# First units behind each norm read the unscaled stream; the norm's factor is applied to their sums

## What is computed

```python
def rmsnorm(x, w):
    y = x * rsqrt(mean(x * x, axis=-1) + EPS)
    return y * w

# A: linear attention with decays
q, fz, i, gate = split(rmsnorm(x, a_norm_w) @ a_w_in);  x = x + (o * silu(gate)) @ a_w_out
# F: keys and values from one norm weight, queries and gates from another
k, v, fz = split(rmsnorm(x, kv_norm_w) @ kv_w);  k = head_rmsnorm(k, k_norm_w)
F = cumsum(log_sigmoid(fz + f_bias))
q, gate = split(rmsnorm(x, b_norm_w) @ b_w_in);  q = head_rmsnorm(q, b_q_norm_w)
x = x + (attention(q, k, v, F) * silu(gate)) @ b_w_out
# C: recurrent unit and attention on 64 selected keys through a latent of 512
xr, q, ckv, qi, ki, wi, gr, ga = split(rmsnorm(x, norm_mix_g) @ w_in)
ckv = rmsnorm(ckv, kv_norm_g);  ki = layernorm(ki)
x = x + mixed @ w_o
# Q: product-key experts: 16 of 16384 experts for each of 8 heads
q = rmsnorm(x, norm_ffn_g) @ peer_wq;  s1, s2 = q1 @ keys1, q2 @ keys2;  top 16, gates
x = x + sum(gate * gelu(h @ u) * v);  out = rmsnorm(x)
```

## Time and profile before

| | |
|---|---|
| median of three timed executions | 3247.22 us |
| the profiled execution | 3245.94 us, its span 3244.2 us |
| PE, PEld | busy 3208.8 and 3052.5 us |
| DVE, ACT, POOL | busy 2346.5, 1671.6 and 7.7 us |
| DMA | 570 MB, 176 GB/s, 49.8% of 16 engines |
| stages (PE, us from the span's start) | start to 23.65; A to 459; OA to 551.17; F to 975; OF to 1067.84; X to 1153; C to 1590; OC to 1684.36; Q to 1787; experts to the end |

### The profile page before, as it was taken

The page is one execution under the profiler, slowest core; times in us unless marked ns, Lnnn a source line. Parts: engine busy times, 40 slices in busy tenths (PEclk is TensorE's granted clock), DMA queues, the critical chain, the costliest instruction groups (busy, mean ns, idle before and its releaser), DMA issues.

```text
span 3244.2 us, 63012 instructions
## 1 busy us (share of the span) xinstructions
PE 3208.8 (99%) x25320; PEld 3052.5 (94%) x25320; DVE 2346.5 (72%) x3759; ACT 1671.6 (52%) x2240; POOL 7.7 (0%) x27
## 2 busy tenths in 40 slices
PE   8999999999999999999999999999999999999998
PEld 7999999999999999999999999998899889987887
DVE  7777667655565675666668998975699558999865
ACT  5454544767684555556544444444444444444444
POOL 0000000000000000000000000000000000000000
PEclk9999999999999999999999999999999999999999
DMA  4444434444444454555445555555555555555554
GB/s 179 148 168 144 166 139 173 171 166 167 156 168 176 165 187 172 177 176 180 163 165 194 176 188 182 182 187 193 192 182 182 195 195 182 182 182 182 183 206 156
DMA packets 99096, 569.96 MB, mean 176 GB/s; under 512 B 9456, under 2 KB 30320, under 8 KB 31600
## 3 DMA queue, kind: packets, MB, share of 16 engines
q1 hardware_dynamic: 98928, 567.58, 49.8%
HBM read 565.45 MB, written 2.10 MB: 175 GB/s over the span
## 4 chain that ended last, share of the span: by engine, by line
PE 90%; DVE 6%; DVEq 1%; DMA 1%; ACT 1%; issue 1%; SPq 0%; ACTq 0%
PE bank L530 20%; PE bank L532 20%; PE bank L531 20%; PE bank L1039 7%; PE bank L1040 7%; PE bank L1041 7%; DVE wl L1542 2%; PE bank L965 1%; PE bank L693 1%; PE bank L879 0%; ACT wh L1070 0%; PE bank L764 0%; PE bank L765 0%; PE bank L640 0%; DMA raw<-w_out_b 0%
## 5 line engine op out<-in xcount | busy, mean ns | idle before, releaser
L530 PE MATMUL bank<-hh,wh 128*128 128x256 f32 x5680 | 1597.8, 281 | 10.9 <-DVE hl L1575 9.1
L531 PE MATMUL bank<-hl,wh 128*128 128x256 f32 x5680 | 1577.3, 278 | 0.0
L532 PE MATMUL bank<-hh,wl 128*128 128x256 f32 x5680 | 1577.3, 278 | 0.0
L1542 DVE TENSOR_TENSOR wl<-raw,wh 128x1024 fp32r<-128x1024 f32 x1052 | 1252.8, 1220 | 357.6 <-ACT wh L1070 349.4
L1070 ACT ACTIVATE wh<-raw 128x1024 fp32r<-128x1024 f32 x1052 | 1052.0, 1050 | 310.7 <-DMA raw<-w_in_a 130.8
L530 PEld LDWEIGHTS bank<-hh,wh 128*128 128x128 f32 x5680 | 1070.6, 188 | 18.5 <-issue 6.8
L531 PEld LDWEIGHTS bank<-hl,wh 128*128 128x128 f32 x5680 | 1071.8, 189 | 3.0 <-issue 1.7
L532 PEld LDWEIGHTS bank<-hh,wl 128*128 128x128 f32 x5680 | 1069.3, 188 | 0.0
L1039 PE MATMUL bank<-wh,ah 128*128 128x512 f32 x1024 | 402.0, 393 | 0.0
L1041 PE MATMUL bank<-wl,ah 128*128 128x512 f32 x1024 | 398.9, 390 | 0.0
L1040 PE MATMUL bank<-wh,al 128*128 128x512 f32 x1024 | 398.5, 389 | 0.0
(11 more groups left out here) (376 smaller groups left out, 2883.7 us busy)
## 6 DMA issues: line engine op xcount, KB each, us to landing
raw<-peer_u SPq DMA_DIRECT2D x128, 1024.0 KB, 4.9
raw<-peer_v SPq DMA_DIRECT2D x128, 1024.0 KB, 4.9
raw<-w_in_c SPq DMA_DIRECT2D x64, 1024.0 KB, 4.9
raw<-w_in_a SPq DMA_DIRECT2D x63, 1024.0 KB, 4.9
raw<-w_kv SPq DMA_DIRECT2D x32, 1024.0 KB, 4.8
raw<-w_in_b SPq DMA_DIRECT2D x32, 1024.0 KB, 4.9
raw<-w_out_a SPq DMA_DIRECT2D x16, 1024.0 KB, 4.9
raw<-w_out_b SPq DMA_DIRECT2D x16, 1024.0 KB, 4.9
```

Of the source, the lines that this page charges most:

```text
L530: eng.matmul(out, h_[:, k, :], high[:, k, :], start=(k == 0), stop=False)
L531: eng.matmul(out, h_[:, k, :], low[:, k, :], start=False, stop=False)
L532: last = eng.matmul(out, low_rows(c, k), high[:, k, :], start=False, stop=(k == KC - 1))
L1542: eng.tensor_tensor(low_half_out(c, half), raw_half(c, half), high_half(c, half).bitcast(F32), ALU.subtract).then_inc(lo_ready, 1)
```

## The change

For each norm there are now two more tiles, `unscaled[name]` (in F `kh` and `kl`): high and low parts of stream times norm weight, without the norm's factor. ACT (`unscaled_high`) and DVE (`unscaled_low`) make them pair by pair during the out-projection, at the start behind the weighing. PE takes them for the first units: four in A, in F the gates' unit and all units of keys and values of all pairs, four in X, four in Q. `norm_sum` comes between the halves of the first unit (`first_unscaled`); `two_products` is gone, and the keep-clock matmuls but for 6 at the start. The factor is applied where the sums are read: a multiplication on DVE of the two banks of A and of the queries of Q, for the gates' unit another; the values of F get it per token as `scale` of ACT's copy, from two transposes of `rstd`; keys and latent are normed anyway, so only their epsilon is divided by the squared factor: `eps_times` makes EPS/rstd^2 from the sum of squares, and DVE adds it to the sum ahead of the root, in F in each pair. In `stream_norm` the scaled parts for the later units follow, with the weights of units 3 and 4 in rounds 2 and 5. In A's first pair the low part of unit 5 stands ahead of `key_decays`, those of 6 and 7 ahead of the two parts of `query_decays`. The small chain for `lb` and `rg_c` moves from behind the first norm to the start. In C's first pair the low parts of `uk` and `uv` are made behind `xc`; in OF `f_norm` moves from chunk 0 to chunk 4 of the second unit; the first load of `uk` and `uv` waits for unit X+4.

```diff
-SPLIT_AT = {"A": 0, "F": 8, "C": 24, "Q": 32}
+SPLIT_AT = {"A": 0, "F": 8, "C": 16, "Q": 24}
...
                 eng.matmul(B[4][:, 0:T], ones[:, :], sq[:, 0, 0:T], start=True, stop=False)
-                keep_clock(3)
                 eng.wait_ge(sq_ready, 8 * NORM_AT[name] + 8)
                 eng.matmul(B[4][:, 0:T], ones[:, :], sq[:, 1, T:2 * T], start=False, stop=True).then_inc(ss_done, 1)
-                keep_clock(15)
+            def first_unscaled(name, c, out):
+                if NORM_AT[name] > 0:
+                    eng.wait_ge(x_next_to_last, NORM_AT[name])
+                product(0, c, out, *unscaled[name], (ul_ready, 8 * NORM_AT[name]), lambda: norm_sum(name))
...
-            for g in range(KC // 2):
+            for g in range(KC // 2 - 2):
                 first_norm_sum(g)
-            keep_clock(14)
+            keep_clock(6)
...
-            two_products(BASE["FG"], [B[5][:, 0:T], B[0][:, 0:T]], kh, kl, SPLIT_AT["F"])
+            first_unscaled("F", BASE["FG"], B[5][:, 0:T])
...
+                if first:
+                    for t in range(NT):
+                        last = eng.transpose(B[7][:, t * P:(t + 1) * P], rstd[:, t * P:(t + 1) * P], ident[:, :])
+                    last.then_inc(s["rtok_done"], 1)
...
-            out_projection("OF", "F", "C", 3, {(0, 6): (f_values,), (1, 0): (f_norm,)})
+            out_projection("OF", "F", "C", 3, {(0, 6): (f_values,), (1, 4): (f_norm,)})
...
-            two_products(u, [latent_bank(0), latent_bank(1)], hh, hl, SPLIT_AT["C"])
-            for c in range(2, RC):
-                product(0, u + c, latent_bank(c), hh, hl)
-            product(0, u + RC, B[2][:, 0:T], hh, hl)
+            first_unscaled("C", u, latent_bank(0))
+            for c in range(1, RC):
+                product(0, u + c, latent_bank(c), uh_c, ul_c)
+            product(0, u + RC, B[2][:, 0:T], hh, hl, (hl_ready, SPLIT_AT["C"]))
...
+            def unscaled_high(name, g):
+                eng.wait_ge(weighed, 8 * NORM_AT[name] + g + 1)
+                eng.activation(chunk(unscaled[name][0], 2 * g, 2), chunk(oT, 2 * g, 2), ACT.Copy).then_inc(uh_ready, 1)
...
+                high_part(0, NORM_UNIT[name] + 2)
+                for g in range(KC // 2):
+                    eng.wait_ge(hf_ready, SPLIT_AT[name] + g + 1)
+                    eng.activation(chunk(hh, 2 * g, 2), chunk(oT, 2 * g, 2), ACT.Copy).then_inc(hh_ready, 1)
+                    if g == 0:
+                        high_part(0, NORM_UNIT[name] + 3)
+                    if g == 3:
+                        high_part(0, NORM_UNIT[name] + 4)
...
-                rsqrt(krs[:, :], B[4][:, :], 1.0 / P).then_inc(s["krs_ready"], 1)
+                eng.wait_ge(s["kvar_ready"], i + 1)
+                rsqrt(krs[:, :], krs[:, :], 1.0 / P, None).then_inc(s["krs_ready"], 1)
...
+            def eps_times(out, n):
+                eng.tensor_scalar(out[:, :], B[4][:, 0:T], n * EPS / D, n * EPS * EPS, ALU.mult, ALU.add)
...
+                eng.wait_ge(s["kss_done"], i + 1)
+                eng.tensor_tensor(krs[:, :].rearrange("p (j t) -> p j t", j=2), B[4][:, :].rearrange("p (j t) -> p j t", j=2),
+                                  epsv_f[:, :].unsqueeze(1).broadcast_to([P, 2, T]), ALU.add).then_inc(s["kvar_ready"], 1)
...
             def a_body(i, first):
...
+                if first:
+                    key_decays(i)
+                    low_part(i, 6)
                 query_decays(i, 0, 3)
-                low_part(i, 6)
+                low_part(i, 7 if first else 6)
```

More of the change, by code:

```diff
@@ L947, in _ @@
                 outs = [query_bank(g, j)[:, j * T:(j + 1) * T] for j in range(2)]
[L948 to L952 removed]
+                for j in range(2):
+                    c = BASE["Q"] + 2 * g + j
+                    if g == 0 and j == 0:
+                        first_unscaled("Q", c, outs[j])
+                    elif g < 2:
+                        product(0, c, outs[j], uh_q, ul_q)
+                    else:
+                        product(0, c, outs[j], hh, hl, (hl_ready, SPLIT_AT["Q"]) if g == 2 and j == 0 else None)
                 if g >= 1:
@@ L1186, in a_body @@
                     eng.activation(osq_a[:, :], B[4][:, :], ACT.Square).then_inc(s["osq_ready"], 1)
-                high_part(i, 5)
-                eng.wait_ge(mm_done, after("A", i, 3))
-                if past_zero(i):
+                if not first:
+                    high_part(i, 5)
+                    eng.wait_ge(mm_done, after("A", i, 3))
                     eng.wait_ge(s["lv_done"], i)
-                eng.activation(q_a[:, :], B[1][:, :], ACT.Copy).then_inc(s["qz_ready"], 1)
+                    eng.activation(q_a[:, :], B[1][:, :], ACT.Copy).then_inc(s["qz_ready"], 1)
                 high_part(i, 6)
@@ L1310, in f_body @@
                 copy_probs(s, i, probT_f)
-                keep_values_tok(s, i, v_f)
+                if past_zero(i):
+                    eng.wait_ge(s["o_done"], i)
+                eng.wait_ge(s["vt_done"], i + 1)
+                for t in range(NT):
+                    last = eng.activation(v_f[:, t, :], B[2][:, t * G:(t + 1) * G], ACT.Copy, scale=rtok[:, t:t + 1])
+                last.then_inc(s["v_ready"], 1)
                 high_part(i, u + 10)
@@ L1573, in low @@
[L1573 to L1595 removed]
+                if name == "F":
+                    eps_times(epsv_f, P)
@@ new lines, in stream_norm @@
+                if name == "C":
+                    eps_times(epsv_c, KV_RANK)
+                low_part(0, NORM_UNIT[name] + 2)
+                eng.drain()
+                for g in range(KC // 2 + 1):
+                    if g < KC // 2:
+                        if weight is None:
+                            last = eng.tensor_tensor(oT[:, 2 * g:2 * g + 2, :], oT[:, 2 * g:2 * g + 2, :],
+                                                     rstd[:, :].unsqueeze(1).broadcast_to([P, 2, T]), ALU.mult)
+                        else:
+                            for c in (2 * g, 2 * g + 1):
+                                last = eng.scalar_tensor_tensor(out=oT[:, c, :], in0=xT[:, c, :], scalar=col(weight, c),
+                                                                in1=rstd[:, :], op0=ALU.mult, op1=ALU.mult)
+                        last.then_inc(hf_ready, 1)
+                    if g >= 1:
+                        eng.wait_ge(hh_ready, SPLIT_AT[name] + g)
+                        eng.tensor_tensor(chunk(hl, 2 * g - 2, 2), chunk(oT, 2 * g - 2, 2), chunk(hh, 2 * g - 2, 2).bitcast(F32),
+                                          ALU.subtract).then_inc(hl_ready, 1)
+                    if g == 2:
+                        low_part(0, NORM_UNIT[name] + 3)
+                    if g == 5:
+                        low_part(0, NORM_UNIT[name] + 4)
+                    if between is not None:
+                        between(g)
@@ L1722, in query_decays @@
                 if first == 0:
+                    if isinstance(i, int) and i == 0:
+                        eng.wait_ge(mm_done, 2 * (BASE["A"] + 4))
+                        eng.tensor_tensor(q_a[:, :].rearrange("p (j t) -> p j t", j=2), B[1][:, :].rearrange("p (j t) -> p j t", j=2),
+                                          rstd[:, :].unsqueeze(1).broadcast_to([P, 2, T]), ALU.mult).then_inc(s["qz_ready"], 1)
+                        eng.drain()
                     eng.wait_ge(s["qz_ready"], i + 1)
@@ L1976, in c_tail, with latent_lows @@
                 eng.tensor_tensor(chunk(oT, i * 2, 2), on_c[:, :], mixr[:, :], ALU.add).then_inc(mixed, 1)
+            def latent_lows(i):
+                for n, (low, full, high) in enumerate(((uk_l, uk, uk_h), (uv_l, uv, uv_h))):
+                    eng.wait_ge(s["kvw_high"], 2 * i + (n + 1))
+                    eng.tensor_tensor(low[:, :, :, :], full[:, :, :, :], high[:, :, :, :].bitcast(F32),
+                                      ALU.subtract).then_inc(s["kvw_low"], 1)
             def c_body(i, first, final=False):
@@ L1982, in c_body @@
                 low_part(i, u + 3)
-                for n, (low, full, high) in enumerate(((uk_l, uk, uk_h), (uv_l, uv, uv_h))):
-                    eng.wait_ge(s["kvw_high"], 2 * i + (n + 1))
-                    eng.tensor_tensor(low[:, :, :, :], full[:, :, :, :], high[:, :, :, :].bitcast(F32),
-                                      ALU.subtract).then_inc(s["kvw_low"], 1)
+                if not first:
+                    latent_lows(i)
                 eng.wait_ge(mm_done, unit(i, BASE["C"] + 1, 2, 2))
```

295 lines of the change are left out of this document (149 added, 146 removed).

## The result

The changed kernel takes 3228.32 us (median of four, 3226.40 to 3230.59) beside 3247.28 for the kernel before: a ratio of 0.9942, 95% interval 0.9929 to 0.9954. A second set of five gave 3227.43 and 0.9944 (0.9931 to 0.9958). The forecast was 3233.6. The profiled execution took 3230.59 us, its span 3228.9.

The account below looks back on a forecast made before the run. TensorE, 99% busy, was taken as the bound, with late DVE or ACT steps deciding its waits at norms. Gains of 16.1 us less 2.5 for the clock gave 13.6, hence 3233.6 us from a profiled 3245.94, range 3225 to 3242.

Parts of the forecast that it names:

- Start: A's first pair: PE's first product at about 21.5, pair ending at 72.0 against 77.49, a gain of 5.5 us.
- F: Norm of F: F+2 waits about 3 us and ends at t+27.8 instead of t+31.5, a gain of 3.65 us.
- The cover of 0.4: F's first pair: query low part ready at t+39.8, wanted by PE at t+40.2, so no loss.
- The added step in the seven later pairs: F's later pairs: the new add of 0.7 us falls in DVE's idle time and costs nothing; uncovered, 4.9 us.
- OF: Out-projection after F: moving `f_norm` 12 matmuls down fills its wait of 1.46 us, a gain of 1.4 us.
- X and Q: Norms of X and Q: PE goes on at t+32.5 and starts key_scores(0) at t+25.2, gains of 2.75 and 2.8 us.
- The waits that were named as signs: PE waits of 2 to 3 us, in X for `csq` and in Q for `keysT`, expected if the forecast was right.
- C: C's first pair: the wait of 0.97 us for `xc` goes, but that for `prob_c` grows by as much; gain 0.
- The sign named: C's first pair: PE waits 1.5 us or more for `prob_c` at L640, expected if the forecast was right.
- The clock: Half clock behind new PE idles: loss of 1.7 us at the start, 0.8 in F, none in X or Q.
- Rival (b): PE falls to half clock at all four new idles and F's cover fails: gain only 5, 3242 us; chance 0.16.
- The root: Each norm: table load takes 1.28 us, so DVE gets the root at about t+4.4; the skill's figure means 1.4 later.

Follow-up runs that it names:

- fillers: Changed kernel with the 18 keep-clock filler matmuls back at each of the norms F, X and Q: 3234.37 us, ratio 0.9961.
- fnorm_back: Changed kernel with `f_norm` back at chunk 0 of OF's second unit: 3237.18 us in one execution.
- keys_first: Changed kernel with ACT copying `keysT` ahead of Q's `stream_norm` instead of behind the last high part: 3227.23 us, ratio 0.994.
- again: The changed kernel run and profiled once more, unchanged: 3227.43 us, ratio 0.9944.
- rounds: Changed kernel with ACT's weight copies for units 3 and 4 one round later in `stream_norm`, behind high parts 1 and 4: 3222.08 us, ratio 0.9923.
- latent_back: Changed kernel with the low parts of `uk` and `uv` in C's first pair ahead of `xc` again: 3228.09 us in one execution.
- before_no_fillers: Kernel before the change, without the 18 filler matmuls in each of the norms F, X and Q: 3252.38 us, ratio 1.0016.
- slow_factor: Changed kernel with two more reciprocals of half a tile ahead of the one in each of the four norms: 3240.82 us, ratio 0.9978.
- squares_first: Changed kernel with ACT squaring all latent chunks in X ahead of the weights of X+5 and X+6: 3230.79 us, ratio 0.9948.

## Why the prediction was right, point by point

**Start.** Right, with two terms a little off. First product 21.09 (said 21.5), unit 3's end 45.42 (45.6). The wait for unit 6's weights is 2.23 (3): DVE's scalings and `key_decays` ended 0.8 earlier than summed. In `fillers`, `fnorm_back` and `keys_first`, whose start is the same, PE came 1 us earlier, waited 3.4 and went on at the same place (59.00 to 59.25): the end of this wait is DVE's, not PE's. Unit 7 waits 0 and 0.22 (0.5). PE ends the pair at 72.07 with a half-clock stretch and in `again` at 70.65 without, where the sum had 72.0 ahead of any loss of clock.

**F.** The sum was t+27.8 for the end of F+2; it ends at 576.54, t+28.0, and at t+27.37 in `fnorm_back`, without the fall of the clock. The waits were 0.30, 2.62 and 0.42, together 3.3 (3). One step of the working does not come out of its own terms: root, epsilon term, eight rounds, three units' weights and 1 us of waits add up to t+25.75 for the last low part, where it says t+27.1; the trace has t+26.49, with 1.26 of waits for ACT. PE's wait was set by the fifth pair, so that this changed little. The cover of 0.4 at the queries' sum held: PE comes at t+40.28 and does not wait. The added step in the seven later pairs costs nothing, as said: from the queries' sum to F's end it took 379.57 against 380.15 and 380.60.

**OF.** 1.4 forecast, 1.26 measured by the wait, 1.2 by undoing it.

**X and Q.** Mechanism and place right, the size 0.3 to 0.4 short: key transposes at t+32.16 (t+32.5), key_scores(0) at t+24.78 (t+25.2). The mis-sized term is the last high part in X, at t+24.85 instead of t+25.2: why it is 0.35 shorter was not traced. The waits that were named as signs, 2 to 3 us, came as 1.35 and 1.15. What I had as bound by ACT's order behind the last high part was the same chain as the rounds; `rounds` shows that it could be shortened at its first link.

**C.** 0 forecast, and `latent_back` shows it: the wait for `prob_c` grew from 0.67 to 1.35 as the wait for `xc` went. The sign named was 1.5 or more.

**The clock.** Right in size, wrong in its reason. The size: at the start 1.2 were taken, and the levels stand at 72.50 with a half-clock stretch and at 71.08 without; in F 0.8 were taken, and the queries' sum stands 0.9 and 1.4 later than in `fnorm_back`. The reason: I took none for X and Q "which follow full stretches". `before_no_fillers` and `slow_factor` have half clock (0.50 to 0.71) behind such stretches. What spared X and Q was the shortness of the idle. These are PE's idles of 1 us and more in all fourteen profiles, between 50 and 3200 us:

| PE's idle, us | how many | half clock during it or within 2.1 us behind it |
|---|---|---|
| 1.03 to 1.66 | 40 | none |
| 1.75 to 2.25 | 8 | 5: after 1.75, 1.99, 2.23, 2.23 and 2.25, not after 1.97, 2.10 and 2.24 |
| 2.43 to 2.63 | 9 | 8: all but 2.54 |
| 3.20 to 4.59 | 8 | 8 |

Rival (b) had the right price for it (2.8; measured 2.6 in Q), but X and Q did not wait 2.0 but 1.35 and 1.15, where no profile has a fall. The Trainium skill, "TensorE: Matmul & The Clock Gate", Part 1, lets the clock follow how busy PE has lately been; the two runs agree with it, and the twin at 59 us shows that the same idle need not have the same effect. That this speaks against dropping the fillers, as the prediction has it, was my inference; `before_no_fillers` bears it out for the kernel before, and `fillers` shows the opposite for the changed one.

**The root.** By the trace's 1.28 for the table load DVE was to have the root at t+4.4 and did, at 552.95, t+4.40. By the figure of "ScalarE: Activation LUTs", section "What ACT_TABLE_LOAD costs", in the Trainium skill it would have been 1.4 later (an estimate), and `slow_factor` shows what such a delay would cost: 1.9 us on this path came out as 1.9 to 2.1 at the start, in X and in Q. The same section gives the load by itself as 1283 ns, and with that the trace agrees (1.28); what it adds for a drain, about 1380 ns, this trace does not show: the load starts at 550.82, right behind a copy that began at 550.51, and the small activation behind the load starts at 552.11.

**The rest.** 13.6 forecast, 19 measured. 3 of the 5.3 us are in the rows above: 1.7 at the start, 0.5 in F, 0.5 in X, 0.3 in Q. Some 2 are left, about what two medians with this rhythm leave open, and not traced to a place; between single profiles the long rhythm moved one stretch alone by 3.8 us, which the prediction had as "some 3 us either way". So the 5.3 us between forecast and result are themselves known to no better than some 3 us.

## What to carry to other kernels

When PE's first work no longer waits for a chain, the wait does not go, it moves to where the chain's end is first needed: list the chain's links and look where the slower engine idles between them. A microsecond taken out at the first link arrived at every later wait (F, X and Q from one edit). Moving the last link is worth something only where nothing else comes right behind it: `keys_first` won 1.3 in Q, `squares_first` nothing in X, for there the wait moved by one instruction. Filler work that keeps the clock is priced by the idle that it fills: 5.5 us won with it where PE would have stood over 4 us, 3.5 or more lost where it stood 1.2 to 2.6. Where parts are worth one to three microseconds of 3200, compare distances between landmarks in two profiles of each kernel; a single total misled by 8 us here.

## What the runs showed of the hardware

Equal instructions run in one of two rhythms, 0.1133 or 0.1176 us a product of 256 columns at full clock, and which one a stretch of dozens to hundreds of products gets differs between executions of one kernel (87 and 91 in the same 10 us). What decides it stays open. And between 50 and 3200 us of the fourteen profiles the lower clock level came with an idle of PE from 1.75 us on, never with one up to 1.66 (40 cases); from 1.75 to 2.25 us it came in 5 of 8 cases, from 2.43 to 2.63 in 8 of 9, from 3.20 in all 8. An idle of 2.23 and one of 2.24 us behind the same instructions had one outcome each; what decides between them stays open.
